# Layer 0's sample queries against their states: states as the stationary side, four query columns as the moving side, summed in the output's own bank

## The chip, the core and the metric

The kernel runs on one core of a Trainium2 chip. The metric is the device time of one execution in microseconds (us), lower is better; three runs of the kernel before gave a median of 1662.35 us. Times in the profile are us from the start of the span, unless a row says ns.

## The reference, cut to what matters

One inference step of a two-layer trunk for 256 prompt tokens and, in the same pass, 8 sample sequences of 4 new tokens each (32 sample tokens). Layer 0 mixes tokens by gated linear attention, layer 1 by an mLSTM; a SwiGLU follows the first, an expert SwiGLU (2 of 8 experts) the second. The change touches one term of layer 0, for the samples alone:

```python
def step(S, blk):                      # S: (batch, head, 128, 256); one chunk of 4 tokens per sample
    ...
    qg = qi * jnp.exp(b)
    ...
    o = jnp.einsum('bhtd,bhdv->bhtv', qg, S) + jnp.einsum('bhts,bhsv->bhtv', A, vi)
    ...
    S_new = jnp.exp(b_end[:, :, 0, :])[..., None] * S + jnp.einsum('bhsd,bhsv->bhdv', k_end, vi)
```

There are 4 heads, a state is 128 x 256 per head and sample, and every sample has its own. The first product of `o` (query times old state) is the one that is changed: 8 samples x 4 heads, a 4 x 128 by 128 x 256 product each. The second product (within the chunk) and the new state stay as they are.

## The kernel before, in words

Each engine has its own instruction stream in program order, and waits on semaphores. `begin(name)` waits until a PSUM bank (8 of them, 512 columns of f32 each) has been read out, `end` says that it is full, `copied(name)` that it has been read. Activations of layer 0 lie feature-major: `q0[:, h, t]` has the 128 features of head h on the partitions and the 288 tokens (256 prompt, then 32 sample) along the columns. Weights come through a ring of 7 slots of 1 MB, which SyncE's queue fills as slots come free. A matmul on f32 operands is issued as two matmul instructions, each with its own weight load (the trace counts x8 where four matmuls are written); one on fp32r operands as one.

The part of layer 0 that matters, on TensorE (PE), in this order:

1. The four prompt chunks: state updates (L1110), scores times values (L1133), queries times running state (L1146), with tiles of the output gate's projection (`r_tile`, L934) between them.
2. `own_part(2, ...)`: for the samples, values as the stationary side and masked scores (32 x 32) as the moving side, into bank `L0o2`, feature-major: eight groups g of 128 output features, 32 token columns each (L1133, 32x32 in the rows). The sum of this bank is left open.
3. For each sample b: four matmuls (L1180), one per head, whose stationary side is `qm0[:, b, h, :]`: 128 features x 32 token columns, zero except for the four columns of sample b. The moving side is the state `Ss[b][:, h, :]`, 256 columns. They add up over the 8 samples in two banks `L0in0` and `L0in1`, token-major (32 tokens on the partitions). Behind them stands `update_sample` (L1122, fp32r): four matmuls that give the state's increment in banks `us{b}a` and `us{b}b`.
4. ScalarE (ACT) copies the two banks to `o_tok0` (L1676, 32 x 512 twice), and TensorE turns them: eight matmuls of `o_tok0` against the identity add them to the open bank `L0o2` (L1187). ACT copies this bank out (L1617), squares the whole output (L1682), and the norm follows on TensorE (L1196) behind `r_tile` 4.

VectorE (DVE) clears `qm0` (L2066) and copies the queries into it (L2068), between the first and the second prompt chunk; the semaphore `qm_ready` says so. Per sample, ACT makes the masked keys `kb` (L1603) two samples ahead, DVE updates the state from the two `us` banks (L1872, four instructions), and GpSimd (POOL) stores it (L762).

Of the kernel before, what the change touches and what calls it, by code (L numbers as in the profile page):

```python
# [21 lines left out]
ACT = mybir.ActivationFunctionType  # L22
AX_X = mybir.AxisListType.X

P = 128
D = 1024
KT = D // P
NP_, NB, NS = 256, 8, 4
NSM = NB * NS
T = NP_ + NSM  # L30
# [38 lines left out]
def bank_plan():  # L69

    uses, turns = {}, [0] * 8

    def use(name, bank):
        uses[name] = (bank, turns[bank])
        turns[bank] += 1

    use("par", 7)
    for kt in range(KT):
        use(f"x{kt}", kt)
    for layer in range(2):  # L80
        l = f"L{layer}"
        use(l + "ss", 3)
        use(l + "rt", 3)
        n = 0

        def pj(name):
            nonlocal n
            use(l + name, n % 3)
            n += 1

        for m in range(4):
            pj(f"q{m}")
        if layer == 0:
            pj("lr")
            pj("k0")
            for m in range(4):
                use(f"L0z{m}", 4 + m)
        else:
            pj("gi")
            pj("gf")  # L100
            pj("k0")
        for m in range(1, 4):
            pj(f"k{m}")
        for s in range(D // COLS):
            for tt in range(TT):
                pj(f"v{s}{tt}")
        if layer == 1:
            use("L1at", 3)
            for j in range(4):
                use(f"L1wb{j}", 4 + j)  # L110
        for tt in range(TT):
            use(l + f"kt{tt}", 4 + tt)
        if layer == 0:
            for tt in range(TT):
                use(l + f"sc{tt}", 3)
        else:
            use("L1nu", 7)
            for tt in range(2):
                for hf in range(2):
                    use(f"L1db{tt}{hf}", 3 + hf)  # L120
                for hf in range(2):
                    use(f"L1sc{tt}{hf}", 5 + hf)
            use("L1db2", 3)
            use("L1sc2", 5)
        for m in range(4):
            pj(f"r{m}")
        for c in range(NC):
            use(l + f"up{c}a", 6)
            use(l + f"up{c}b", 7)
        for tt in range(2):  # L130
            use(l + f"o{tt}a", 4)
            use(l + f"o{tt}b", 5)
        use(l + "o2", 4)
        if layer == 1:
            use("L1den", 3)
        use(l + "in0", 0)
        if layer == 0:
            use(l + "in1", 1)
        for b in range(NB):
            pair = (6, 7) if b % 2 == 0 else (2, 3) if layer == 0 else (1, 2)  # L140
            use(l + f"us{b}a", pair[0])
            use(l + f"us{b}b", pair[1])
        use(l + "r4", 0)
        use(l + "ns", 5)
        use(l + "r5", 1)
        for h in range(GH if layer == 0 else MH):
            use(l + f"nb{h}", (2, 0, 1)[h % 3])
        use(l + "r6", 6)
        use(l + "r7", 7)
        for m in range(8):  # L150
            use(l + f"w{m}", 3 + m % 5)
        if layer == 0:
            use("Fss", 3)
            for f in range(FFT):
                base = 0 if (f % 2 == 0) else 4
                use(f"Fg{f}", base)
                use(f"Fu{f}", base + 1)
            for m in range(8):
                use(f"Fw{m}", [2, 3, 6, 7][m % 4])
    use("Mlog", 2)  # L160
    for kt in range(KT):
        use(f"Mx{kt}", kt % 2)
    use("Mrank", 0)
    use("Mga0", 1)
    use("Mga1", 3)
    use("Mgt", 7)
    return uses, turns
# [11 lines left out]
def trunk_kernel(nc, ins, outs):  # L179
# [5 lines left out]
    with ExitStack() as ctx:  # L185
# [90 lines left out]
        def area(at, *dims, rows_=P, of=None):  # L276

            n = 1
            for d in dims:
                n *= d  # L280
            v = (work if of is None else of)[0:rows_, at:at + n]
            if len(dims) == 2:
                v = v.rearrange("p (a b) -> p a b", a=dims[0])
            if len(dims) == 3:
                v = v.rearrange("p (a b c) -> p a b c", a=dims[0], b=dims[1])
            return v
# [14 lines left out]
        v3 = area(23552, D, rows_=STACK, of=work_split)  # L301
        kb = area(9216, 2, QK, rows_=STACK, of=work_split)
        k3_0 = area(3456, QK, rows_=STACK, of=work_split)
        qm0_mem = area(1152, NB * (GH * NSM + NS))
        qm0 = qm0_mem[:, 0:NB * GH * NSM].rearrange("p (b h t) -> p b h t", b=NB, h=GH)
        mx_hi = area(6912, KT, STACK, of=work_split)
        mx_lo = area(7680, KT, STACK, of=work_split)
        kx = area(8448, 4, STACK)
        rowx = area(8832, 2, STACK, rows_=MH)
        rbx = area(24416, STACK, rows_=1)  # L310
        o_tok0 = area(2304, D, rows_=NSM)
        Ss = [area(at, GH, GDV) for at in (18048, 19072, 20096, 21120, 22144, 13056, 14848, 17024)]
        k3_1 = area(22528, QK, rows_=STACK, of=work_split)
        qm1_mem = area(4608, NB * (MH * NSM + NS))
# [193 lines left out]
        def full(name):  # L508

            b, k = uses[name]  # L510
            return bank_full[b], k + 1

        def copied(name):

            b, k = uses[name]
            return bank_free[b], k + 1
# [361 lines left out]
        def _(pe):  # L878
            taken = [0]

            def begin(name):

                b, k = uses[name]
                if k:
                    pe.wait_ge(bank_free[b], k)
                return psum[b]

            def end(mm, name):
                mm.then_inc(bank_full[uses[name][0]], 1)
# [280 lines left out]
            inter0(3, True)  # L1170
            pe.wait_ge(*copied("L0sc2"))
            own_part(2, NSM, lambda g: P0s[:, g // 2, :], ["L0o2"])
            pe.wait_ge(qm_ready, 1)
            for s in range(D // COLS):
                pe.wait_ge(*copied(f"L0v{s}2"))
            inter = [begin(f"L0in{x}") for x in range(2)]
            for b in range(NB):
                pe.wait_ge(S_loaded[b], 16)
                for h in range(GH):
                    mm = pe.matmul(inter[h // 2][0:NSM, (h % 2) * GDV:(h % 2 + 1) * GDV], qm0[:, b, h, :], Ss[b][:, h, :],  # L1180
                                   start=(b == 0 and h % 2 == 0), stop=(b == NB - 1), skip_group_check=True)
                    if b == NB - 1 and h % 2:
                        end(mm, f"L0in{h // 2}")
                update_sample("L0", b, 0)
            for g in range(8):
                pe.wait_ge(*copied(f"L0in{g // 4}"))
                mm = pe.matmul(psum[uses["L0o2"][0]][:, g * NSM:(g + 1) * NSM], o_tok0[:, g * P:(g + 1) * P], ident[0:NSM, 0:NSM],  # L1187
                               start=False, stop=True, skip_group_check=True)
            end(mm, "L0o2")


            r_tile("L0", 4)
# [154 lines left out]
            for g in range(MH):  # L1347
                mm = pe.matmul(den[0:MH, NP_:T], head_col[:, g, :], qn[:, g, :], start=False, stop=True, skip_group_check=True)
            end(mm, "L1den")
            pe.wait_ge(qm_ready, 2)  # L1350
            for s in range(D // COLS):
                pe.wait_ge(*copied(f"L1v{s}2"))
            inter = begin("L1in0")
# [174 lines left out]
        def _(ac):  # L1528
# [8 lines left out]
            def take(name):  # L1537
                b, k = uses[name]
                ac.wait_ge(bank_full[b], k + 1)
                return psum[b]  # L1540

            def free(ins_, name):
                ins_.then_inc(bank_free[uses[name][0]], 1)
# [128 lines left out]
            ac.wait_ge(*copied("L0kt2"))  # L1672
            for b in range(NB):
                sample_keys("L0", b, 0)
            for x in range(2):
                free(ac.activation(o_tok0[:, x * 512:(x + 1) * 512], take(f"L0in{x}")[0:NSM, :], ACT.Copy), f"L0in{x}")  # L1676
            output("L0", o0, 2)
            ac.wait_ge(*copied("L0o2"))
            ac.wait_ge(*copied("L0o1b"))
# [170 lines left out]
        def _(ve):  # L1850
            chain = [0]

            def step(ins_):

                chain[0] += 1
                ins_.then_inc(v_chain, 1)
                ve.wait_ge(v_chain, chain[0])
# [194 lines left out]
            for c in range(NC):  # L2052
                for half, x in enumerate("ab"):
                    name = f"L0up{c}{x}"
                    bk = take(name)
                    if c == 0:
                        free_step(ve.tensor_copy(S0[:, 1, 2 * half:2 * half + 2, :], bk[:, :].rearrange("p (h v) -> p h v", h=2)), name)
                        continue
                    for a in range(2):
                        h = 2 * half + a  # L2060
                        ins_ = stt(S0[:, (c + 1) % 2, h, :], S0[:, c % 2, h, :], eb[:, h, c:c + 1], bk[:, a * 256:(a + 1) * 256],
                                   ALU.mult, ALU.add)
                    free_step(ins_, name)
                if c == 0:
                    ve.wait_ge(*full("L0sc2"))
                    step(ve.memset(qm0_mem, 0.0))  # L2066
                    out = qm0_mem.rearrange("p (b x) -> p b x", b=NB)[:, :, 0:GH * NSM].rearrange("p b (h t) -> p b h t", h=GH)[:, :, :, 0:NS]
                    ve.tensor_copy(out, q0[:, :, NP_:T].rearrange("p h (b i) -> p b h i", b=NB)).then_inc(qm_ready, 1)  # L2068
            for b in range(NB):
                ve.wait_ge(S_loaded[b], 16)  # L2070
                for half, x in enumerate("ab"):
# [458 lines left out]
```

## Time and profile before

| | |
|---|---|
| runs | 1670.69, 1656.62, 1662.35 us; median 1662.35 |
| profiled execution | 1660.21 us, its span 1657.9 us |
| mean granted TensorE clock | 0.979 of full speed |
| PE busy | 1614.0 us (97%), 8546 matmuls |
| DVE, ACT, POOL busy | 1191.0, 980.7, 123.9 us |
| the sample stretch on PE (first L1180 to the last L1187) | 127.97 to 151.50 us of the chain |

The engines' rows in the trace name the line, the operation, output<-input, the stationary side (for TensorE) and the moving side, and a count. TensorE's granted clock is given as a share of 2.4 GHz: 1.00 is 2.4 GHz, 0.50 is 1.2 GHz. The end of a matmul row is modelled, so the time that a matmul takes in a series is read from start to start.

### The profile page before, as it was taken

The numbers are of one execution on the slowest core, as the hardware profiler recorded it, in microseconds if no ns is written. First come the engines' busy times: TensorE is split into PE (matmuls) and PEld (weight loads), VectorE is DVE, ScalarE is ACT, GpSimd is POOL, SyncE is SP. The second block draws the span as 40 slices with busy tenths as digits, with TensorE's granted clock in tenths as the row PEclk, the third lists the DMA queues.
The fourth block names the chain that finished last, engine by engine and source line by source line (L and its number), as shares of the span: only waits on it lengthen the run. The fifth ranks groups of instructions, "written<-read, shape, count | busy, mean of one in ns | idle before, by whom it ended". The sixth has DMA issues, their size and how long they took to land.

```text
span 1657.9 us, 22845 instructions
## 1 busy us (share of the span) xinstructions
PE 1614.0 (97%) x8546; PEld 1249.8 (75%) x8546; DVE 1191.0 (72%) x1166; ACT 980.7 (59%) x837; POOL 123.9 (7%) x173
## 2 busy tenths in 40 slices
PE   8999999999998998999999999999999999999996
PEld 6986799999897867777677677677677677777774
DVE  5633457653645443888888888888888888888887
ACT  5513343333522232777877877777777778778774
POOL 2011000000101030300000000000000000000010
PEclk9999999999997989999999999999999999999998
DMA  8444345445442154799999999999999999999992
GB/s 253 131 148 170 121 153 174 153 157 173 138 140 77 40 94 144 273 383 381 361 378 376 363 380 365 378 373 369 381 369 366 381 372 354 392 374 351 394 367 108
DMA packets 233110, 449.96 MB, mean 271 GB/s; under 512 B 15868, under 2 KB 82480, under 8 KB 233056
## 3 DMA queue, kind: packets, MB, share of 16 engines
q1 hardware_dynamic: 224752, 422.32, 71.3%
q0 software_dynamic: 7632, 24.54, 5.3%
q10 hardware_dynamic: 672, 2.36, 0.4%
q8 instruction: 37, 0.61, 0.2%
q14 instruction: 17, 0.14, 0.0%
HBM read 434.62 MB, written 14.57 MB: 271 GB/s over the span
## 4 chain that ended last, share of the span: by engine, by line
PE 95%; DVE 3%; ACT 1%; issue 1%; POOL 0%; DVEq 0%; POOLq 0%
PE bank L940 25%; PE bank L942 25%; PE bank L941 25%; PE bank L934 8%; PE bank L1465 1%; PE bank L1180 1%; PE bank L1029 1%; PE bank L1110 1%; PE bank L925 1%; PE bank L1146 1%; PE bank L1133 1%; PE bank L1122 1%; PE bank L1402 0%; PE bank L1290 0%; PE bank L1292 0%
## 5 line engine op out<-in xcount | busy, mean ns | idle before, releaser
L2401 DVE TENSOR_TENSOR w_lo<-ring,w_hi 128x2048 fp32r<-128x2048 f32 x337 | 771.0, 2290 | 122.2 <-ACT w_hi L1787 119.8
L1787 ACT ACTIVATE w_hi<-ring 128x2048 fp32r<-128x2048 f32 x337 | 645.4, 1918 | 225.1 <-PE bank L942 224.2
L940 PE MATMUL bank<-w_hi,xg_hi 128*96 128x512 f32 x896 | 355.8, 397 | 1.0 <-DVE xg_lo L2411 1.0
L942 PE MATMUL bank<-w_hi,xg_lo 128*96 128x512 f32 x896 | 354.0, 395 | 0.0
L941 PE MATMUL bank<-w_lo,xg_hi 128*96 128x512 f32 x896 | 351.7, 393 | 0.0
L940 PE MATMUL bank<-work_split 128*128 128x288 f32 (+2 forms) x840 | 246.3, 293 | 3.3 <-DVE work_split L2114 2.6
L942 PEld LDWEIGHTS bank<-w_hi,xg_lo 128*96 128x96 f32 x896 | 144.5, 161 | 62.8
L941 PE MATMUL bank<-work_split 128*128 128x288 f32 x648 | 191.0, 295 | 0.0
L942 PE MATMUL bank<-work_split,ring_lo 128*128 128x288 f32 x648 | 190.9, 295 | 0.0
L940 PEld LDWEIGHTS bank<-w_hi,xg_hi 128*96 128x96 f32 x896 | 144.6, 161 | 61.2 <-DVE w_lo L2401 2.0
L941 PEld LDWEIGHTS bank<-w_lo,xg_hi 128*96 128x96 f32 x896 | 145.1, 162 | 59.9
L940 PEld LDWEIGHTS bank<-work_split 128*128 128x128 f32 (+1 forms) x840 | 156.8, 187 | 5.3 <-DVE work_split L2114 2.9
L1578 ACT ACTIVATE work_split<-ring 128x2048 fp32r<-128x2048 f32 (+1 forms) x49 | 91.8, 1875 | 90.5 <-PE bank L942 84.2
L942 PEld LDWEIGHTS bank<-work_split,ring_lo 128*128 128x128 f32 x648 | 122.5, 189 | 0.0
L941 PEld LDWEIGHTS bank<-work_split 128*128 128x128 f32 x648 | 122.3, 189 | 0.2
L2093 DVE TENSOR_TENSOR ring_lo<-ring,work_split 128x2048 fp32r<-128x2048 f32 (+1 forms) x34 | 75.5, 2225 | 35.8 <-ACT work_split L1578 35.8
L942 PE MATMUL bank<-w_hi,aT_lo 128*96 128x512 f32 x256 | 101.1, 395 | 0.0
L940 PE MATMUL bank<-w_hi,aT_hi 128*96 128x512 f32 x256 | 100.8, 394 | 0.0
L941 PE MATMUL bank<-w_lo,aT_hi 128*96 128x512 f32 x256 | 100.4, 392 | 0.0
L940 PE MATMUL bank<-w_hi,hT_split 128*96 128x512 f32 x192 | 76.5, 399 | 0.0
L941 PE MATMUL bank<-w_lo,hT_split 128*96 128x512 f32 x192 | 75.6, 394 | 0.0
L942 PE MATMUL bank<-w_hi,hT_split 128*96 128x512 f32 x192 | 75.2, 392 | 0.0
(424 smaller groups left out, 1829.2 us busy)
## 6 DMA issues: line engine op xcount, KB each, us to landing
ring<-in_moe_w_gu_dram SPq DMA_DIRECT2D x225, 1024.0 KB, 6.1
ring<-in_moe_w_down_dram SPq DMA_DIRECT2D x112, 1024.0 KB, 6.1
ring<-in_ffn_w_gu_dram SPq DMA_DIRECT2D x22, 1024.0 KB, 5.1
ring<-in_gla_w_in_dram SPq DMA_DIRECT2D x12, 1024.0 KB, 9.7
ring<-in_mlstm_w_in_dram SPq DMA_DIRECT2D x12, 1024.0 KB, 5.2
ring<-in_ffn_w_down_dram SPq DMA_DIRECT2D x8, 1024.0 KB, 5.1
out_dram<-work POOLq DMA_DIRECT2D x9, 512.0 KB, 3.3
ring<-in_gla_w_out_dram SPq DMA_DIRECT2D x4, 1024.0 KB, 5.0
```

The costliest lines, as they stand in the source:

```text
L925: mm = pe.matmul(bk[:, 0:T], ones[:, :], hT[:, kt, :], start=(kt == 0), stop=(kt == KT - 1))
L934: mm = pe.matmul(bk[0:m, 0:T], w[:, kt, c:c + m], src[:, kt, :], start=(kt == 0), stop=(kt == n - 1))
L940: pe.matmul(out, w_hi_, x_hi, start=first, stop=False, skip_group_check=True)
L941: pe.matmul(out, w_hi_, x_lo, start=False, stop=False, skip_group_check=True)
L942: return pe.matmul(out, w_lo_, x_hi, start=False, stop=last, skip_group_check=True)
L1029: mm = pe.matmul(banks[m][:, 0:T], w[:, kt, m * P:(m + 1) * P], src[:, kt, :], start=(kt == 0), stop=(kt == KT - 1))
L1110: mm = pe.matmul(bk[:, h * 256:(h + 1) * 256], kz[:, c, g * P:(g + 1) * P], v_tok[:, c // 2, g * 256:(g + 1) * 256], start=True, stop=True)
L1122: mm = pe.matmul(bk[:, h * 256:(h + 1) * 256], kb[:, b % 2, g * P:(g + 1) * P], v3[:, g * 256:(g + 1) * 256], start=True, stop=True)
L1578: ac.activation(hi, raw, ACT.Copy).then_inc(fhi_ready, 1)
L1787: ac.activation(w_hi[:, j % SPLIT, :], src, ACT.Copy).then_inc(whi_ready, 1)
L2093: ve.tensor_tensor(lo, raw, hi.bitcast(F32), ALU.subtract).then_inc(flo_ready, 1)
L2401: ve.tensor_tensor(w_lo[:, j % SPLIT, :], src, w_hi[:, j % SPLIT, :].bitcast(F32), ALU.subtract)\
```

## The change

The state becomes the stationary side. For sample b and each of eight groups g of 128 output features (head g // 2, half g % 2), one matmul has 128 x 128 of the state as its stationary side and the sample's four query columns of `q0` as its moving side. Its 128 x 4 result is added to the four columns of sample b in the group g of bank `L0o2`, which is open from `own_part`. So the output comes feature-major at once. The cleared and filled `qm0`, the banks `L0in0` and `L0in1`, their copies on ACT, `o_tok0` and the eight turning matmuls are gone. `update_sample` stays behind each sample, and the last of the new matmuls, before the last `update_sample`, marks `L0o2` full.

```diff
-        use(l + "in0", 0)
-        if layer == 0:
-            use(l + "in1", 1)
+        if layer == 1:
+            use("L1in0", 0)
...
             own_part(2, NSM, lambda g: P0s[:, g // 2, :], ["L0o2"])
-            pe.wait_ge(qm_ready, 1)
             for s in range(D // COLS):
                 pe.wait_ge(*copied(f"L0v{s}2"))
-            inter = [begin(f"L0in{x}") for x in range(2)]
+            bk = psum[uses["L0o2"][0]]
             for b in range(NB):
                 pe.wait_ge(S_loaded[b], 16)
-                for h in range(GH):
-                    mm = pe.matmul(inter[h // 2][0:NSM, (h % 2) * GDV:(h % 2 + 1) * GDV], qm0[:, b, h, :], Ss[b][:, h, :],
-                                   start=(b == 0 and h % 2 == 0), stop=(b == NB - 1), skip_group_check=True)
-                    if b == NB - 1 and h % 2:
-                        end(mm, f"L0in{h // 2}")
+                t = NP_ + b * NS
+                for g in range(8):
+                    c = g * NSM + b * NS
+                    mm = pe.matmul(bk[:, c:c + NS], Ss[b][:, g // 2, g % 2 * P:(g % 2 + 1) * P], q0[:, g // 2, t:t + NS],
+                                   start=False, stop=True, skip_group_check=True)
+                if b == NB - 1:
+                    end(mm, "L0o2")
                 update_sample("L0", b, 0)
-            for g in range(8):
-                pe.wait_ge(*copied(f"L0in{g // 4}"))
-                mm = pe.matmul(psum[uses["L0o2"][0]][:, g * NSM:(g + 1) * NSM], o_tok0[:, g * P:(g + 1) * P], ident[0:NSM, 0:NSM],
-                               start=False, stop=True, skip_group_check=True)
-            end(mm, "L0o2")
...
-            for x in range(2):
-                free(ac.activation(o_tok0[:, x * 512:(x + 1) * 512], take(f"L0in{x}")[0:NSM, :], ACT.Copy), f"L0in{x}")
+
             output("L0", o0, 2)
...
-                if c == 0:
-                    ve.wait_ge(*full("L0sc2"))
-                    step(ve.memset(qm0_mem, 0.0))
-                    out = qm0_mem.rearrange("p (b x) -> p b x", b=NB)[:, :, 0:GH * NSM].rearrange("p b (h t) -> p b h t", h=GH)[:, :, :, 0:NS]
-                    ve.tensor_copy(out, q0[:, :, NP_:T].rearrange("p h (b i) -> p b h i", b=NB)).then_inc(qm_ready, 1)
```

Layer 1's wait for its own `qm_ready` counts to 1 in place of 2; the areas of `qm0` and `o_tok0` are no longer named.

On TensorE the sample part before, from the samples' own part (L1133, 128x32) to the two instructions behind it (rows give the output's shape; four of the eight samples are left out):

```order
514 L1133 MATMUL bank<-work 128x32 x8
515 L1180 MATMUL bank<-work 32x256 x4
516 L1122 MATMUL bank<-work_split 128x256 x4
517 L1180 MATMUL bank<-work 32x256 x4
518 L1122 MATMUL bank<-work_split 128x256 x4
...
529 L1180 MATMUL bank<-work 32x256 x4
530 L1122 MATMUL bank<-work_split 128x256 x4
531 L1187 MATMUL bank<-ident,work 128x32 x8
532 L934 MATMUL bank<-hT,ring 128x288 x8
533 L1196 MATMUL bank<-work,head_col 8x288 x8
```

And the same part now (line numbers are those of the changed file: L1131 is the own part, L1179 the new matmuls, L1120 the update, L932 `r_tile`, L1190 the norm):

```order
514 L1131 MATMUL bank<-work 128x32 x8
515 L1179 MATMUL bank<-work 128x4 x8
516 L1120 MATMUL bank<-work_split 128x256 x4
517 L1179 MATMUL bank<-work 128x4 x8
518 L1120 MATMUL bank<-work_split 128x256 x4
...
529 L1179 MATMUL bank<-work 128x4 x8
530 L1120 MATMUL bank<-work_split 128x256 x4
531 L932 MATMUL bank<-hT,ring 128x288 x8
532 L1190 MATMUL bank<-work,head_col 8x288 x8
```

Nothing has changed its place: each sample's four matmuls of 256 columns have become eight of 4 columns, and the eight turning matmuls behind the last sample are gone, so that `r_tile` follows the last update.

## Rows read from the trace of the kernel before

**Rows 1.** The page, parts 1 and 4: PE's busy time, the chain's shares.

```profile
PE 1614.0 (97%) x8546; PEld 1249.8 (75%) x8546; DVE 1191.0 (72%) x1166; ACT 980.7 (59%) x837; POOL 123.9 (7%) x173
PE 95%; DVE 3%; ACT 1%; issue 1%; POOL 0%; DVEq 0%; POOLq 0%
```

**Rows 2.** The chain that ended last, 126 to 156 us: start, length, what, count.

```profile
126.07 1.90 PE bank L1133 x16
127.97 2.83 PE bank L1180 x8
130.80 1.16 PE bank L1122 x4
131.96 1.92 PE bank L1180 x8
133.88 0.67 PE bank L1122 x4
...
149.60 1.90 PE bank L1187 x16
151.50 4.08 PE bank L934 x16
```

**Rows 3.** Busy time by stretch: PE, PEld, DVE, ACT, POOL, clock, DMA share, GB/s.

```profile
125.27:128.68 3.41, 3.41 (x28) 2.98 (x27) 0.00 (x0) 2.35 (x4) 1.50 (x2) 1.00 1.05 337
128.69:132.04 3.35, 3.35 (x11) 1.62 (x9) 0.37 (x1) 0.04 (x1) 0.00 (x0) 0.50 0.92 323
132.10:149.50 17.40, 17.40 (x84) 9.17 (x82) 11.19 (x29) 5.34 (x8) 4.83 (x7) 1.00 0.53 182
```

**Rows 4.** Timeline of PE, 512 to 529 us (layer 1): start, length, instruction.

```profile
512.35 1.05 PE L1302 MATMUL bank<-ones,work 128*128 128x1 f32 x8
513.34 0.38 PE L1303 MATMUL bank<-batch_of,work 32*128 32x8 f32 x2
...
515.33 1.87 PE L1302 MATMUL bank<-ones,work 128*128 128x1 f32 x8
517.12 0.59 PE L1303 MATMUL bank<-batch_of,work 32*128 32x8 f32 x2
...
521.26 3.64 PE L1292 MATMUL bank<-work 128*128 128x128 f32 x16
524.73 4.05 PE L934 MATMUL bank<-hT,ring 128*128 128x288 f32 x16
```

**Rows 5.** Busy time by stretch, layer 1, around the rows of group 4.

```profile
511.00:514.30 3.30, 3.30 (x28) 3.18 (x26) 0.00 (x0) 1.78 (x2) 0.00 (x0) 1.00 0.00 0
514.40:521.20 6.80, 6.80 (x31) 6.58 (x30) 0.90 (x2) 0.00 (x0) 0.00 (x0) 0.50 0.01 2
521.20:524.60 3.40, 3.40 (x16) 3.35 (x16) 1.92 (x3) 1.70 (x2) 0.00 (x0) 0.50 0.00 0
524.70:528.00 3.30, 3.30 (x16) 2.62 (x16) 1.88 (x3) 0.64 (x1) 0.00 (x0) 1.00 0.00 0
```

**Rows 6.** Busy time by stretch, layer 1: wide matmuls (L934) from 608.33 at the low clock.

```profile
608.33:613.30 4.97, 4.97 (x12) 3.54 (x12) 0.53 (x2) 0.00 (x0) 0.00 (x0) 0.50 0.79 95
613.50:618.60 5.10, 5.10 (x22) 4.00 (x22) 0.88 (x2) 0.50 (x1) 1.00 (x5) 1.00 0.46 150
```

**Rows 7.** Groups by line, 100 to 420 us: busy us, mean ns, idle before, releaser.

```profile
L1187 PE MATMUL bank<-ident,work 32*128 32x32 f32 x16 | 2.0, 272 | 0.0
L2066 DVE MEMSET work<- 128x1056 f32 x1 | 0.9, 938 | 0.3 <-DVE work L2057 0.3
L2068 DVE COPY work<-work 128x128 f32<-128x128 f32 x1 | 0.2, 228 | 0.0
L1676 ACT ACTIVATE work<-bank 32x512 f32<-32x512 f32 x2 | 1.2, 586 | 3.0 <-PE bank L1180 3.0
```

**Rows 8.** Timeline, one sample's work off PE, 136 to 138 us.

```profile
136.63 0.75 POOL L762 DMA_DIRECT2D out_dram<-work  x1 [1.61 <-DVE work L1872]
136.93 1.66 DVE L1872 SCALAR_TENSOR_TENSOR work<-work,eb,bank 128x256 f32<-128x256 f32 x4 [0.85 <-PE bank L1122]
137.10 0.72 ACT L1603 ACTIVATE work_split<-work_split,batch_of 96x512 fp32r<-96x512 f32 x1 [1.79 <-PE bank L1122]
```

**Rows 9.** The instructions of L1292: ns min/median/max, first and last start, forms.

```profile
L1292 PEld LDWEIGHTS bank<-work x48: 106/333/334, 503.4 to 529.8; 128*128 128x128 f32 x32, 128*32 128x32 f32 x16
```

More of the change, by code:

```diff
@@ L303, in trunk_kernel @@
         k3_0 = area(3456, QK, rows_=STACK, of=work_split)
-        qm0_mem = area(1152, NB * (GH * NSM + NS))
-        qm0 = qm0_mem[:, 0:NB * GH * NSM].rearrange("p (b h t) -> p b h t", b=NB, h=GH)
         mx_hi = area(6912, KT, STACK, of=work_split)
@@ L310, in trunk_kernel @@
         rbx = area(24416, STACK, rows_=1)
-        o_tok0 = area(2304, D, rows_=NSM)
         Ss = [area(at, GH, GDV) for at in (18048, 19072, 20096, 21120, 22144, 13056, 14848, 17024)]
@@ L1349, in _ @@
             end(mm, "L1den")
-            pe.wait_ge(qm_ready, 2)
+            pe.wait_ge(qm_ready, 1)
             for s in range(D // COLS):
```

## Prediction

> **What bounds the kernel.** I read the shares first: PE is busy 97% of the span and holds 95% of the chain that ended last [rows 1]. So I went on to the chain at the changed place. From the samples' own part to the norm it never leaves PE: 8 times L1180 and L1122, then the turn L1187, then `r_tile` [rows 2]. What counts is the time that PE takes from 127.97 to 151.50, that is **23.53 us**. A steady sample costs 1.92 + 0.67 = 2.59 us by the row shown, and 2.51 us in the six rows left out (1.84 + 0.67). The first is dearer, 2.83 + 1.16, because the granted clock is at 1.2 GHz from 128.69 to 132.04 [rows 3]. Off PE a sample takes 1.66 us of DVE, 0.72 us of ACT and 0.75 us of POOL, each with idle time that ends with PE's own L1122 [rows 8]: they follow PE. I then looked for matmuls as thin as the new ones. The nearest are in layer 1: L1302, f32, stationary 128 x 128, **one** moving column [rows 4], with the clock around them [rows 5].
>
> **The change, part by part.** It removes:
> - 64 instructions of L1180 (8 per sample, 0.23 us each in 1.84 us) and the 16 of L1187, 1.90 us [rows 2]. All on the path.
> - Two ACT copies of 0.59 us and the DVE clear and copy, 0.94 + 0.23 us [rows 7]. Worth nothing. ACT's copies end while PE works on the last L1122, and L1187 starts with no idle time before it [rows 7]. DVE's two were done 25 us before their reader, with work of PE's own between. If that cover were gone they would be worth 1.2 us each.
> - The waits for `qm_ready` and the two banks: PE has no idle time in front of L1180 in the chain [rows 2], so they are worth nothing.
>
> It adds 64 matmuls, 128 instructions, 16 per sample, each with its own 128 x 128 weight load. Columns do not price them: L1302 with one column takes (513.34 - 512.35) / 8 = 0.124 us at 2.4 GHz and (517.12 - 515.33) / 8 = 0.224 us at 1.2 GHz [rows 4]. PEld is busy 3.18 of 3.30 us there [rows 5], so the weight loads are the price, and four columns in place of one change nothing. The bounds: L1187's 1.90 / 16 = 0.119 us from below at the high clock [rows 2], and twice 0.124 = 0.248 us from above at the low one.
> - At 2.4 GHz a sample costs 16 x 0.124 + 0.67 = 2.65 us, about what it costs now. Eight make 21.2 us.
> - At 1.2 GHz it costs 16 x 0.224 + 1.16 = 4.74 us; the 1.16 is L1122 in the first sample, at that clock [rows 2, 3]. Eight make 37.9 us.
>
> So **the clock decides**. It was granted at 2.4 GHz while L1302 and L1303 ran from 511.0 to 514.3, with PE and PEld busy throughout, and then at 1.2 GHz through more of them, through 16 instructions with 8 rows (L1290), and through 3.4 us of full 128 x 128 by 128 ones. It rose at 524.6 [rows 4, 5]. In the changed stretch the same kind of instruction fills 2.0 of every 2.65 us, and it comes behind a stretch after which the clock fell anyway (L1133 with 32 rows; 28 matmuls, then 0.50) [rows 3]. Before, the wide L1180 and L1122 that followed brought it back at 132.04. Now only L1122 is left wide, a quarter of the time. I take it that the clock falls at about 128.7 as before and stays down until `r_tile`.
>
> The Trainium skill speaks the other way here: "TensorE: Matmul & The Clock Gate", section "Why this matters for your kernels", warns of idle gaps between bursts of matmuls, and this stretch has none. By that rule the clock stays up and the change saves about 2 us. The rows at 511.0 to 514.3 had no gap either, and the clock fell behind them [rows 5].
>
> **The sum.** Sample stretch: the 0.71 us from 127.97 to 128.68 run at the high clock and do the work of 0.71 x 4.74 / 2.65 = 1.27 us at the low one, so 37.9 - 0.56 = 37.4 us. Less the 23.5 us of now: **+13.9 us**. Behind it `r_tile` begins at the low clock. In layer 1 L934 began at 608.33 with the clock down and had it back only behind 613.30, 5.0 us, in which half of that time is lost [rows 6]; L1292's 3.4 us at 521.2 is the short case [rows 5]. That makes 1.7 to 2.5 us; I take +1.8, as where the rise falls is chance. Total **+15.7 us**. The profiled execution would go from 1660.2 to 1675.9 us. It is 2.1 us under the median, so the forecast for a median is 1662.35 + 15.7 = **1678 us**.
>
> What is late next: ACT's read of `L0o2`, its squares and the norm hang on `L0o2` alone. That is now full before the last L1122 and not behind L1187, and `r_tile` 4 (4.08 us) lies between, so they get slack, not delay. DVE (1.66 us per sample) has 4.74 us. No queue is passed: POOL's loads and stores keep their order and get later by PE's delay, SP's weight loads too, and PE works unbroken from its ring behind this place. So the delay goes through to the end.
>
> **The rivals.**
> - *The clock stays up* (the rule above; ends on the other side of zero). Mechanism: weight loads, or the L1122 between, keep the clock granted at 2.4 GHz over the sample stretch. 8 x 2.65 = 21.2 against 23.5 us: 2.3 us saved, up to 2.9 with L1187's 0.119. Time about 1660 us. It decides as long as no more than one of the eight samples runs at the low clock: each that does costs 4.74 - 2.65 = 2.1 us, which is the whole saving. For it: layer 1 has 8 samples of its own without a fall, but with wide moving sides. Against: rows 4 and 5. 0.08.
> - *The clock comes and goes*, half the samples at each level: 8 x 3.70 = 29.6 us, +6, with 0.9 for `r_tile`: about 1669 us. 0.06.
> - *The weight load is not overlapped.* With four columns to hide under, each instruction might wait for its whole load, 0.333 us at the low clock by L1292's PEld [rows 9]: 16 x 0.333 + 1.16 = 6.5 us, eight 51.9, +28.4 + 1.8: 1692 us. L1302's spacing of 0.224 us at that clock speaks against it [rows 4]. 0.04.
> - *Columns are the price after all.* Were 4 columns 4/256 of L1180's 0.23 us, the new matmuls would cost next to nothing: 8 x (0.06 + 0.67) = 5.8 us, 17.7 us saved, 1645 us. Rows 4 refute it nearly: one column costs 0.124 us. 0.02. The Trainium skill's "Back-to-back issue gap" on the same page gives about 60 cycles for 1 to 64 columns, an estimate of 128 x 25 ns = 3.2 us for all of them; the same section adds that a stream with weight loads is set by both, and the trace agrees with that part.
>
> **The numbers.** The forecast, the low clock throughout, has 0.80. Its own spread: instructions at 0.214 (0.01 less than L1302's, as between single rows) to 0.248 us, the bound above, give -1.3 to +3.1 us; L1122 at twice 0.67 in place of 1.16 gives +1.4; where the clock's fall and rise lie in a run, 1.5 us either way; and the three runs of before lie 14 us apart, so a median is good to some 4 us. That is 1669 to 1688 us. For 8 in 10 the range takes in the half-way rival: **1667 to 1689 us**. About 1% (16.6 us, the limit 1679) is what a measurement of this kernel tells from no change. The forecast lies just under it, with the larger part of its spread above: of its 0.80 I give 0.38 to over 1% slower and 0.42 to within. Slower 0.38 + 0.04 (loads not overlapped) = 0.42; same 0.42 + 0.08 + 0.06 = 0.56; faster 0.02.
>
> **What would show it.** In the profile after: 128 instructions of 128*128 128x4 f32 in place of L1180's 64; start to start 0.22 us for most of them; L1120 behind each group 1.2 us; granted clock 0.50 from about 129 to about 168 us; stretch from the own part to `r_tile` 37 us; the first `r_tile` over 5 us; everything behind it shifted by 15 to 16 us with its lengths unchanged. Wrong if the clock stands at 1.00 within the samples (the first rival), if the spacing is 0.3 us or more (the third), or if the shift is smaller at the end than at 170 us, since then something behind it had slack.

## The result, and the profile after

20 runs of the changed kernel have a median of 1673.63 us (1669.98 to 1678.14), 20 runs of the kernel before one of 1661.12 us (1656.62 to 1671.28). The ratio is **1.0068** (95% interval 1.0056 to 1.0081): 11.3 us slower by the ratio, 12.5 us by the medians. The forecast was +15.7 us, a median of 1678 us within 1667 to 1689 us, with "within 1%" as the likeliest outcome; the measured ratio is within 1%. All 20 runs of the changed kernel have a mean granted clock of 0.963 to 0.970, and its profiled execution (1670.35 us, 0.970) is one of the seven shortest, 3.3 us under the median; ten others lie at 1674.38 to 1678.14 us with 0.963 to 0.966, and none of those was profiled.

The chain that ended last, in the changed kernel, at the same place as [rows 2] (start, length, what, count; L1131 is the samples' own part, L1179 the new matmuls, L1120 the update, L932 `r_tile`, L1190 and L1196 the norm, L1027 the output projection):

```profile
126.28 1.90 PE bank L1131 x16
128.18 2.64 PE bank L1179 x16
130.82 1.06 PE bank L1120 x4
131.88 3.21 PE bank L1179 x16
135.09 1.06 PE bank L1120 x4
...
160.69 1.06 PE bank L1120 x4
161.75 6.37 PE bank L932 x16
168.11 3.98 PE bank L1190 x16
...
178.62 7.96 PE bank L932 x32
186.58 7.76 PE bank L1027 x32
```

The stretch from the first new matmul to `r_tile` is 161.75 - 128.18 = 33.57 us, against 23.53. A steady sample costs 3.21 + 1.06 = 4.27 us, against 2.51. The weight loads of such a sample (PEld) start 0.213 us apart, the 16 narrow ones (134.88 - 131.47 = 3.41 us) and the four of the update (135.73 - 134.88 = 0.85 us) alike:

```profile
131.47 3.53 PEld L1179 LDWEIGHTS bank<-work 128*128 128x128 f32 x16
134.88 0.97 PEld L1120 LDWEIGHTS bank<-work_split 96*128 96x128 f32 x4
135.73 3.53 PEld L1179 LDWEIGHTS bank<-work 128*128 128x128 f32 x16
```

The busy time by stretch, with the granted clock as the third number from the right, answers to [rows 3]:

```profile
125.50:129.00 3.50, 3.50 (x32) 3.39 (x31) 0.00 (x0) 2.34 (x4) 1.50 (x2) 1.00 1.06 334
129.15:161.50 32.35, 32.35 (x153) 32.35 (x153) 11.67 (x29) 5.08 (x8) 5.26 (x7) 0.50 0.39 138
161.54:166.60 5.06, 5.06 (x12) 3.63 (x12) 1.54 (x4) 2.37 (x4) 0.75 (x1) 0.50 0.42 146
166.80:170.00 3.20, 3.20 (x15) 1.44 (x14) 0.00 (x0) 1.78 (x2) 0.00 (x0) 1.00 0.02 5
```

From 129.15 to 161.50 the clock is 1.2 GHz, with PE and its weight loads busy 32.35 of 32.35 us: nothing waits, everything is slow. It stays down through about 5 us of `r_tile`, which takes 6.37 us in place of 4.08. How the difference builds up along the chain, in starts: `r_tile` 151.50 to 161.75, +10.25; the norm behind it +12.54 (168.11 against 155.57); the output projection +10.85 (186.58 against 175.73). The last step gives 1.7 us back, in this pair of profiles: before, the 32 instructions of `r_tile` ahead of the projection hit a fall of the clock of their own and took 9.64 us, here 7.96. At these three rows of the kernel before:

```profile
155.57 3.98 PE bank L1196 x16
166.09 9.64 PE bank L934 x32
175.73 7.76 PE bank L1029 x32
```

The spans, 1657.9 and 1668.6 us, differ by 10.7: from there on next to nothing is gained or lost.

### The profile page after: what moved, and what is told of

Read it like the earlier page. It is cut to its first block, busy times and chain, and to the rows that moved or that the text cites. A ratio compares the mean times of both kernels' runs of the same rounds, so it can differ in the third digit from the quotient of the medians.

```text
span 1668.6 us, 22935 instructions
## 1 busy us (share of the span) xinstructions
PE 1624.5 (97%) x8594; PEld 1270.0 (76%) x8594; DVE 1189.9 (71%) x1164; ACT 979.6 (59%) x835; POOL 123.9 (7%) x173
## 4 chain that ended last, share of the span: by engine, by line
PE 95%; DVE 3%; ACT 1%; issue 1%; POOL 0%; DVEq 0%; POOLq 0%
PE bank L938 25%; PE bank L940 25%; PE bank L939 25%; PE bank L932 8%; PE bank L1179 2%; PE bank L1459 1%; PE bank L1027 1%; PE bank L1108 1%; PE bank L1120 1%; PE bank L923 1%; PE bank L1144 1%; PE bank L1131 1%; PE bank L1396 0%; PE bank L1284 0%; PE bank L1286 0%
```

## The experiments

In each diff the changed kernel is the base, unless the text says otherwise. Rates are read from start to start. Where one run was made, its time stands alone, and the reading rests on its trace.

**128 moving columns in place of 4** (`e1_cols128`), into a bank aside:

```diff
-                    mm = pe.matmul(bk[:, c:c + NS], Ss[b][:, g // 2, ...], q0[:, g // 2, t:t + NS], ...)
+                    mm = pe.matmul(aside[:, g % 4 * 128:(g % 4 + 1) * 128], Ss[b][:, g // 2, ...], q0[:, g // 2, T - 128:T], ...)
```

> The changed kernel, but all of the 64 new matmuls save the last take 128 columns of the queries in place of 4 and write to a bank aside, so the samples' first term is left out of the output. Same 128 instructions, same 128 weight loads of 128x128, 32 times the columns. Theory (the clock is the loss): the clock is granted at 2.4 GHz over most of the samples, a steady sample takes 16 x 0.111 + 0.67 = about 2.4 us in place of 4.27, the stretch up to r_tile about 21 us in place of 33.6 (one fall at its start may stay), r_tile 3.9 to 4.1 us in place of 6.4, the whole about 1659 us, faster than the change though it computes more. Rival (the loads of the states cost that by themselves at any clock, or the adding into one bank does): the stretch stays at 33.6 us or grows, the whole at 1673 us or above.

Measured: 1656.78 us (8 runs), ratio to the kernel before 0.9975 (0.9964 to 0.9986). PE's timeline (start, length, line, stationary and moving side), first and steady samples:

```profile
131.37 3.39 PE L1180 MATMUL bank<-work 128*128 128x128 f32 x16
134.51 0.72 PE L1119 MATMUL bank<-work_split 96*128 96x256 f32 x4
135.07 1.95 PE L1180 MATMUL bank<-work 128*128 128x128 f32 x16
...
137.34 1.95 PE L1180 MATMUL bank<-work 128*128 128x128 f32 x16
```

And its busy time by stretch:

```profile
130.90:134.20 3.30, 3.30 (x16) 3.24 (x16) 0.00 (x0) 0.25 (x1) 0.49 (x1) 0.50 1.05 344
134.51:150.90 16.39, 16.39 (x147) 16.39 (x146) 11.59 (x28) 4.82 (x8) 4.52 (x6) 1.00 0.55 194
```

The clock falls at about 130.8 us, ahead of the first sample (before the change it fell 0.7 us into it), and comes back at about 134.3, near the first sample's end. A sample is then 137.34 - 135.07 = 2.27 us in place of 4.27, the stretch 150.91 - 131.37 = 19.5 us, and the whole is 16.9 us faster than the changed kernel, with 32 times the columns and the same instructions and loads. That is the forecast of the clock's theory (1659 us, a stretch of 21) and speaks against the other: the loss is the clock's. The next run has the same bank aside with fewer columns.

**32 columns** (`e2_cols32`), the same edit with 32.

> As the run before, but with 32 columns (all sample tokens) in place of 128, into the bank aside; the samples' first term is left out of the output. Theory of the clock: in between; before the change 16 such instructions (L1133, 32x32) stood ahead of a fall, so I expect the clock down for most of the stretch and 30 to 34 us for it. If more columns bring the clock back, 20 to 24 us. The rival says 33.6 us or more.

Measured: 1678.4 us in one run, the stretch 161.61 - 127.32 = 34.3 us, at 1.2 GHz throughout:

```profile
127.32:161.61 34.29, 34.29 (x162) 34.29 (x161) 11.71 (x29) 5.47 (x10) 5.55 (x8) 0.50 0.41 142
```

As leaned to: 32 columns do not bring it back, and cost no more than 4 (4.26 us a sample, by the chain). The bank aside is the same as with 128 columns, so it was not the bank that made that run faster.

**One column** (`e3_cols1`): `bk[:, c:c + 1]` and `q0[:, g // 2, t:t + 1]`.

> The changed kernel with one query column per matmul in place of 4: three of the four sample columns of the term are left out. Theory (the weight load is the price of each instruction): start to start 0.213 us at 1.2 GHz as with 4 columns, stretch 33.6 us. Rival (L1302's 0.224 us of the forecast is what one column costs): 0.224 us, a sample 16 x 0.224 + 1.06 = 4.6 us, stretch 37 us.

Measured: 1671.02 us in one run. The timeline of PE, a steady sample:

```profile
131.78 3.41 PE L1179 MATMUL bank<-work 128*128 128x1 f32 x16
135.05 1.20 PE L1120 MATMUL bank<-work_split 96*128 96x256 f32 x4
136.05 3.41 PE L1179 MATMUL bank<-work 128*128 128x1 f32 x16
```

136.05 - 131.78 = 4.27 us, the same as with 4 columns. So L1302's 0.224 us, from which I priced, is not what one column costs here. It was measured on groups of 8 that alternate with two instructions of L1303; why it is 0.011 us more there, no run shows.

**Half of each weight load** (`e4_half_load`): `Ss[b][..., g % 2 * P:g % 2 * P + 64]`, 64 output partitions.

> The changed kernel with 64 of each 128 state columns as the stationary side: half the output features of the term are left out. Theory (price by the columns of the weight load): start to start 0.107 us at 1.2 GHz, a sample 16 x 0.107 + 4 x 0.213 = 2.6 us, stretch 20 to 21 us although the clock stays at 1.2 GHz. Rival (a price per instruction, whatever it loads): 0.21 us and 33.6 us as before.

Measured: 1660.68 us in one run. The timeline of PE:

```profile
130.85 1.87 PE L1179 MATMUL bank<-work 128*64 128x4 f32 x16
132.65 1.22 PE L1120 MATMUL bank<-work_split 96*128 96x256 f32 x4
133.80 1.87 PE L1179 MATMUL bank<-work 128*64 128x4 f32 x16
```

(132.65 - 130.85) / 16 = 0.113 us, half of the full load's; the clock is at 0.50 from 130.85 to 151.30. The stretch is 151.39 - 128.67 = 22.7 us, 2 us above the forecast, as a sample is 2.95 us and not 2.6: the update takes 1.15 us and not 0.85, and the load engine then stands idle for 0.22 us before the next narrow group. What the update waits for was not tried.

```profile
133.80 1.78 PEld L1179 LDWEIGHTS bank<-work 128*64 128x64 f32 x16 [0.22 <-issue]
```

For the narrow matmuls the columns of the load are the price.

**The masked queries in four copies** (`e9_copies`), base the kernel before. Its `qm0`, `L0in0` and `L0in1` stay; the state is the stationary side, the own part goes into the same two banks, and nothing is turned:

```diff
+            def columns(g):
+                return inter[g // 4][:, g % 4 * P:(g % 4 + 1) * P].rearrange("p (r t) -> p r t", r=4)
...
-                for h in range(GH):
-                    mm = pe.matmul(inter[h // 2][0:NSM, ...], qm0[:, b, h, :], Ss[b][:, h, :], ...)
+                for g in range(8):
+                    mm = pe.matmul(columns(g), Ss[b][:, g // 2, g % 2 * P:(g % 2 + 1) * P],
+                                   qm0[:, b, g // 2, :].unsqueeze(1).broadcast_to([P, 4, NSM]), ...)
...
-                free(ac.activation(o_tok0[:, x * 512:(x + 1) * 512], take(f"L0in{x}")[0:NSM, :], ACT.Copy), f"L0in{x}")
+                free(ac.activation(o0[:, 4 * x:4 * x + 4, NP_:T],
+                                   take(f"L0in{x}")[:, :].rearrange("p (g r t) -> p g r t", g=4, r=4)[:, :, 0, :], ACT.Copy), f"L0in{x}")
```

> The state stays the stationary side, nothing is left out. The moving side is the masked queries of the kernel before (32 columns, zero but for sample b's four), repeated four times by a stride of zero: 128 columns into two banks, of which ACT reads the first copy; the samples' own part goes into the same banks, so there is no turn. From the run with 128 columns: a steady sample 2.26 us at 2.4 GHz, the stretch up to r_tile about 19.5 to 21 us with one fall at its start, against 23.5 before the change and 33.6 with it; about 3 to 4 us faster than the kernel before, 1656 to 1658 us. Rival (what made the run with 128 columns fast was that its sum was left out, not its clock: repeated reads with stride zero, or adding on over the samples, cost more): stretch 24 us or more, no gain on the kernel before.

Measured: **1655.63 us** (8 runs), ratio to the kernel before **0.9968 (0.9956 to 0.9980)**: 5 us under the kernel before, an interval clear of no change but only 0.3%, and 18 us under the changed kernel. Its chain (L1177 is the own part, L1185 the samples, L1121 the update, L933 `r_tile`):

```profile
126.99 1.90 PE bank L1177 x16
128.88 1.98 PE bank L1185 x16
130.87 0.48 PE bank L1121 x4
131.34 1.79 PE bank L1185 x16
...
147.19 3.88 PE bank L933 x16
```

A sample is 1.79 + 0.48 = 2.27 us, the stretch 147.19 - 128.88 = 18.3 us against 23.5, and the clock stays at 2.4 GHz through all of it in this profile:

```profile
128.88:147.19 18.31, 18.31 (x162) 18.31 (x162) 11.72 (x29) 4.97 (x9) 4.90 (x8) 1.00 0.69 240
```

**The same with one copy** (`e11_one_copy`), base the run above:

```diff
-                    mm = pe.matmul(columns(g), Ss[b]..., qm0[:, b, g // 2, :].unsqueeze(1).broadcast_to([P, 4, NSM]), ...)
+                    mm = pe.matmul(columns(g)[:, 0, :], Ss[b]..., qm0[:, b, g // 2, :], ...)
```

> The kernel with four copies of the masked queries, with one copy: 32 moving columns in place of 128 in the samples' 128 instructions, nothing else differs and nothing is left out. Theory of the clock: it stays at 1.2 GHz over the samples, a sample takes 20 loads x 0.213 = 4.27 us in place of 2.26, the stretch 32 to 34 us, the whole about 1672 us, 15 us slower than with four copies though it moves a quarter of the columns. Rival (the gain lay in the banks or in the missing turn): 1656 us as with four copies.

Measured: 1672.31 us (5 runs), ratio to the kernel before 1.0065 (1.0039 to 1.0090). Its chain:

```profile
131.79 3.25 PE bank L1185 x16
135.04 1.01 PE bank L1121 x4
136.05 3.25 PE bank L1185 x16
```

And its clock, with PE and PEld as busy as in the run above:

```profile
127.60:161.65 34.05, 34.05 (x160) 34.05 (x161) 11.88 (x29) 5.50 (x9) 5.27 (x7) 0.50 0.41 140
```

A sample is 4.26 us again, and the stretch 161.65 - 127.25 = 34.4 us against 18.3. Two kernels with the same result, the same instructions, banks and loads, and only the width of the moving side apart, lie 16.7 us apart, 16.1 of them in this stretch, and the one that moves a quarter of the columns is the slower. This is the cleanest pair of the runs. It shows, with the runs with 128 and 32 columns, that the wide moving side keeps the clock up or brings it back, and the thin one does not. It does not show that the thin ones start the fall: in 12 of the 13 profiles at hand the clock falls between 126.8 and 131 us, around the own part and the first sample, the kernel before and the run with 128 columns among them.

**The own part in four copies too** (`e10_copies_own`): `P0s[:, g // 2, :].unsqueeze(1).broadcast_to([NSM, 4, NSM])` as its moving side.

> As the run before, and the samples' own part (32x32 matmuls, behind which the clock falls in the kernel before) repeats its 32 moving columns four times too. If moving columns alone bring the clock back, the fall at about 129 us is gone and 1 to 1.5 us more are saved, a stretch of 18 to 19 us. If the 32 rows that these matmuls use count too, the fall stays and the time is that of the run before.

Measured: 1654.72 us (9 runs), ratio 0.9966 (0.9954 to 0.9977), the same as the run with four copies alone. In its profile the clock fell behind the own part all the same, in the samples' first 3.3 us (busy time by stretch):

```profile
128.30:131.60 3.30, 3.30 (x18) 3.30 (x18) 0.00 (x0) 0.00 (x0) 0.00 (x0) 0.52 1.06 359
132.17:148.00 15.83, 15.83 (x141) 15.83 (x141) 11.55 (x29) 4.96 (x9) 4.69 (x7) 1.00 0.55 192
```

So wide own-part matmuls do not rule the fall out, and the copies gain nothing that these runs can tell. That the 32 rows are the reason is not shown: the profile of the run before, whose own part has the same 32 rows and only 32 columns, has no fall at all at this place. With one profile of each, the fall may be chance in both.

**Wide matmuls between the samples** (`e6_r45_between`, `e12_r45_timed`): `r_tile` 4 and 5 in pieces.

```diff
+                for m in range(2):
+                    mm = pe.matmul(pieces[m][:, 0:T], r_weights[0][:, b, m * P:(m + 1) * P], hT[:, b, :], start=(b == 0), stop=(b == NB - 1))
+                    ...
                 update_sample("L0", b, 0)
```

> The changed kernel with the 16 wide matmuls (32 instructions, 288 columns) of r_tile 4 and 5 put between the samples, two behind each sample's narrow ones; r_tile 6 and 7 move up in their place. Nothing is left out. At 2.4 GHz samples and tiles together take 8 x (2.26 + 0.97) = 26 us, at 1.2 GHz 8 x (4.27 + 1.94) = 50 us. If the clock comes back, the whole is about 1660 us; if it stays down because narrow ones still hold two thirds of the time, the wide ones are slow too and it is 1680 us or more. I lean to the second: it came back only behind stretches of wide matmuls alone.

Measured: 1657.91 us in one run; the chain (L1181 samples, L1186 pieces, L1120 update):

```profile
127.42 3.51 PE bank L1181 x16
130.92 2.13 PE bank L1186 x4
133.05 0.85 PE bank L1120 x4
133.90 1.71 PE bank L1181 x16
135.61 1.08 PE bank L1186 x4
136.69 0.47 PE bank L1120 x4
137.16 1.68 PE bank L1181 x16
```

I had leaned the wrong way: the clock was back from the second sample on, and samples and tiles took 156.61 - 127.42 = 29.2 us. The loads of the 4-column matmuls then start (138.67 - 136.88) / 16 = 0.112 us apart:

```profile
136.88 1.88 PEld L1181 LDWEIGHTS bank<-work 128*128 128x128 f32 x16
138.67 0.79 PEld L1186 LDWEIGHTS bank<-hT,ring 128*128 128x128 f32 x4
```

The same kernel in 11 runs:

> The changed kernel with r_tile 4 and 5 between the samples again, to be timed: the one look had the clock back from the second sample on and 1657.9 us. If that is how it goes in every run, the median is 1656 to 1659 us, 14 to 17 us under the changed kernel, and 2 to 5 us under the kernel before. If it depends on where the clock's fall lies in a run, some runs lie near 1680 us and the median moves up.

Measured: 11 runs from 1658.02 to 1669.79 us, median 1663.97, ratio to the kernel before 1.0010 (0.9989 to 1.0032). Four lie at 1658.0 to 1659.2, one at 1660.8, six at 1664.0 to 1669.8, where the 8 runs of the four copies lie within 3.1 us. That fits a clock that comes back in some runs early, in others late or not at all, which was my second case. The mean granted clock of each run goes the same way: 0.978 in the four shortest, 0.971 to 0.974 in the six longest. But both profiles show it back after the first sample, and none of the longer runs was profiled, so that the clock is lost in this stretch is argued and not shown.

**One tile between** (`e5_r4_between`), half as many wide ones.

> The changed kernel with r_tile 4 alone between the samples: one wide matmul (2 instructions) behind each sample's narrow ones. Half the wide work of the run with two tiles. If the clock comes back: 8 x (2.26 + 0.49) = 22 us for samples and tile, the whole about 1658 us; if it stays down: 8 x (4.27 + 0.97) = 42 us, about 1674 us. After the run with two tiles I have no row that tells which; the run with 32 columns, where it stayed down, is the nearer, so I lean to 42 us.

Measured: 1674.61 us in one run; samples and tile take 169.77 - 128.83 = 40.9 us, near the 42 that I leaned to, and the clock stays at 0.50:

```profile
130.00:165.00 35.00, 35.00 (x149) 32.99 (x149) 10.71 (x26) 4.33 (x6) 4.52 (x6) 0.50 0.33 118
```

**The turn alone** (`e7_before_one_turned`), base the kernel before: `for g in range(7, 8)` over L1187.

> The kernel before with one of the eight turning matmuls (L1187): seven eighths of the samples' first term are left out. Forecast for this term: 14 of 16 instructions of 0.119 us, so the stretch from the first L1180 to r_tile is 1.7 us shorter than 23.5, and nothing else moves. Rival (the turn is covered by other work): no change of the stretch.

Measured: 1658.5 us in one run. The chain:

```profile
131.72 1.84 PE bank L1180 x8
...
149.27 0.01 issue
149.28 0.41 PE bank L1187 x2
149.69 4.08 PE bank L934 x16
```

Seven steady samples and the turn take 149.69 - 131.72 = 17.97 us, in the kernel before 151.50 - 131.96 = 19.54: 1.57 us less, 1.7 were expected. Of the 1.57, 0.09 is the first of these samples, which the kernel before still ran partly at the low clock; the turn itself goes from 1.90 to 0.42 us, 1.48 us less. The turn was on the path and its removal is a gain, which the clock outweighs.

## Why the prediction was right, and where it was off

The forecast median of 1678 us lies 4.4 us above the measured 1673.63: 1.2 us because the 20 runs of the kernel before have a lower median than its first three, 3.2 us because the change cost 12.5 us and not 15.7.

- *PE holds the chain; DVE, ACT and POOL follow*: right. PE has no idle time from 129.15 to 161.50, and the shift at the projection is that of the span (10.85 and 10.7 us). One sign that I had named for being wrong did appear: the shift is smaller at the end (10.7 us) than at 168 us (12.54). It was not slack in the work behind: it is the fall of the clock that only the kernel before met, below.
- *The clock falls at about 128.7 and stays down until `r_tile`*: right. It fell at 129 and stayed at 1.2 GHz to 166.6, inside `r_tile`. That it is the cause of the loss is shown by the pair with one and four copies (16.7 us apart) and by the run with 128 columns (16.9 us under the changed kernel).
- *The rule that was weighed against it*: idle gaps were not needed. The Trainium skill, "TensorE: Matmul & The Clock Gate", section "Why this matters for your kernels", warns of them; here PE was busy without a gap, by its rows, for 32.35 us at 0.50. The trace does not agree that avoiding gaps is enough.
- *The price of an instruction at 1.2 GHz*: the step that was too high. "16 x 0.224 + 1.16 = 4.74 us" is 3.21 + 1.06 = 4.27 us. I had taken the two prices from separate rows. In truth the sample is one unbroken row of 20 weight loads, 16 + 4, of 4.27 / 20 = 0.213 us each, just under the lower bound of 0.214 that I had given, and with up to 32 columns what a narrow matmul streams adds nothing. The one-column run gives the same 4.27 us, and the run with half loads halves the narrow ones' share. The stretch is 33.57 us and not 37.4: 3.8 us of the error.
- *The price at 2.4 GHz* was too high in the same way: 0.124 us, where the loads in the run with wide matmuls between start 0.112 us apart. The Trainium skill, "TensorE: Matmul & The Clock Gate", section "LDWEIGHTS (loading the stationary operand)", gives 128 columns / 1.2, 107 ns, for a load: at 2.4 GHz the trace agrees within 5% (0.112 us), at 1.2 GHz it does not (0.213 us). Had the clock stayed up, the change would have saved about 23.5 - 18.3 = 5.2 us and not 2.3. That is an estimate: it takes the stretch of the run with four copies, which kept its clock and has the same loads. So the first rival would have been right on its sign and short by more than half on its size.
- *`r_tile` at the low clock, +1.8*: 6.37 - 4.08 = 2.3 us, inside the 1.7 to 2.5 that the prediction gave.
- *The rest keeps its length*: not quite. 1.7 us came back at the fall before the projection. Which small fall a run meets varies: these tiles took 9.64 or 9.65 us in the profiles of the kernel before, of 32 columns, one column, half loads, own copies, one copy and one turned group, and 7.96 us in those of the changed kernel, of 128 columns and of four copies. The sum of these, 10.04 + 0.21 + 2.29 - 1.69 = 10.85 us, is the profile's; the forecast's 15.7 differs by 3.8 for the samples, -0.5 for `r_tile`, 1.7 for this fall and -0.2 for the start. The 1.7 us are the luck of this profile as far as is known: by the medians the change costs 12.5 us, and where its longer runs lose the rest no profile shows; their lower clock (0.963 to 0.966) says only that more of it was run at the low level.
- *The turn, worth 1.90 us, and ACT's and DVE's parts, worth nothing*: 1.5 us of 1.7 in the run with one turned group; the second part was not tried alone.
- *The third rival* (loads not overlapped) is refuted: the loads' rows are 0.323 us long on average, but they overlap, and from start to start it is 0.213 us, not 0.333. *The fourth* (price by columns) too: 1, 4 and 32 columns cost the same.

## What to carry to other kernels

Making the moving side thin saved nothing here once the weight load of 128 columns was the longer of the two, and it left the clock at half for all that stood around it, without a single idle gap in the trace. Before such a swap, look for the thinnest matmuls that the kernel already has and read the granted clock behind them; price the new ones as a count of weight loads in one row, not from a short group's mean. If the loads bound the row anyway, try a fuller moving side: here four copies of the same columns cost no time of their own and were 16.7 us faster than one, though only 5 us (0.3%) under the kernel before the change.

## What the runs showed that I had not expected

- With two tiles between the samples the clock came back in both profiles, with one it did not, and the timed runs of the two-tile form spread over 11.8 us. A form that works in some runs alone is not a fix; the 8 runs with four copies lie close together (1653.98 to 1657.12 us).
- The clock fell behind the own part's 32-row matmuls in one profile with 128 moving columns, and did not in one with 32. The fall at this place is not explained by these runs.
- A full load rate binds at either clock: 0.213 us at 1.2 GHz with 1, 4 and 32 moving columns, 0.112 us at 2.4 GHz with 4 and, in the runs with 128 columns and four copies, with 128.
